# The causal mask of attention is added by a bf16 product instead of an fp32 product

## The reference

```
for blk in range(S // Q_BLOCK):            # two blocks of 128 queries
    q0 = blk * Q_BLOCK; q1 = q0 + Q_BLOCK
    s = einsum('bqhcd,bkhcd->bhcqk', q[:, q0:q1], k[:, :q1]) * ATTN_SCALE
    mask = arange(q1)[None, :] <= arange(q0, q1)[:, None]
    s = where(mask, s, -inf)
    a = softmax(s, axis=-1)
    a = a[:, :, 0] - lam * a[:, :, 1]      # 8 heads, two maps each
    outs.append(einsum('bhqk,bkhe->bqhe', a, v[:, :q1]))
```

## Time and profile before

| What | Value |
|---|---|
| Median of three executions | 1508.78 us |
| Lowest, highest | 1506.01, 1510.01 us |
| Profiled execution: span from first to last instruction | 1507.1 us (the page gives no other time of this execution) |
| Mean granted TensorE clock | 0.969 |
| TensorE busy (matmul, weight load) | 1451.4 us (96%), 1214.6 us (81%) |
| VectorE, ScalarE, GpSimd busy | 1156.3 us, 928.3 us, 129.1 us |
| DMA | 423.00 MB, mean 281 GB/s |

### The profile page before, as it was taken

How to read it: one execution, slowest core, us unless ns; L and a number is a source line. 1 busy time by engine, 2 the same in 40 slices (tenths; PEclk the granted TensorE clock), 3 DMA queues, 4 the chain that set the end, 5 groups by cost and what they waited for, 6 DMA issues and landing times.

```text
span 1507.1 us, 19735 instructions
## 1 busy us (share of the span) xinstructions
PE 1451.4 (96%) x7300; PEld 1214.6 (81%) x7300; DVE 1156.3 (77%) x894; ACT 928.3 (62%) x796; POOL 129.1 (9%) x129
## 2 busy tenths in 40 slices
PE   6789899999988999999999999999999999999998
PEld 5676689999877888888888888888888888888876
DVE  4764455444666888998988888898898889889875
ACT  4433443343445777777777767777777776777763
POOL 6650152000131000000000000000000000000000
PEclk9985699999999999999999999999999999999999
DMA  9440065555544997999999999999999999999970
GB/s 337 146 167 0 27 198 188 189 193 179 179 163 158 334 347 274 355 359 377 337 358 372 333 352 374 346 351 373 338 358 352 380 330 355 377 339 345 368 292 28
DMA packets 191374, 423.00 MB, mean 281 GB/s; under 512 B 6752, under 2 KB 30304, under 8 KB 191328
## 3 DMA queue, kind: packets, MB, share of 16 engines
q1 hardware_dynamic: 190880, 421.55, 78.2%
q0 software_dynamic: 448, 0.82, 0.2%
HBM read 421.30 MB, written 1.05 MB: 280 GB/s over the span
## 4 chain that ended last, share of the span: by engine, by line
PE 87%; DVE 6%; ACT 2%; POOL 2%; issue 1%; DMA 1%; SPq 0%; POOLq 0%; ACTq 0%; DVEq 0%
PE ps L264 26%; PE ps L266 25%; PE ps L265 25%; PE ps L732 2%; DVE w_lo L235 2%; PE ps L541 2%; PE ps L611 2%; PE ps L543 1%; POOL rstd L1476 1%; ACT w_hi L229 1%; PE ps L748 1%; DVE wide L1167 1%; DVE xs L1085 1%; DMA raw<-in_attn_w_qkv_dram 1%; ACT y_hi L1014 0%
## 5 line engine op out<-in xcount | busy, mean ns | idle before, releaser
L235 DVE TENSOR_TENSOR w_lo<-raw,w_hi 128x2048 fp32r<-128x2048 f32 (+1 forms) x393 | 881.1, 2257 | 210.5 <-ACT w_hi L229 209.5
L229 ACT ACTIVATE w_hi<-raw 128x2048 fp32r<-128x2048 f32 x393 | 752.1, 1916 | 201.6 <-PE ps L266 199.0
L264 PE MATMUL ps<-w_hi,xe_hi 128*128 128x512 f32 x896 | 356.2, 398 | 1.8 <-DVE w_lo L235 1.8
L266 PE MATMUL ps<-w_hi,xe_lo 128*128 128x512 f32 x896 | 350.3, 391 | 0.0
L265 PE MATMUL ps<-w_lo,xe_hi 128*128 128x512 f32 x896 | 349.9, 390 | 0.0
L264 PE MATMUL ps<-w_hi,h_t_hi 128*128 128x512 f32 x536 | 210.6, 393 | 3.4 <-DVE h_t_lo L1250 1.8
L266 PE MATMUL ps<-w_hi,h_t_lo 128*128 128x512 f32 x536 | 209.1, 390 | 0.0
L265 PE MATMUL ps<-w_lo,h_t_hi 128*128 128x512 f32 x536 | 208.9, 390 | 0.0
L264 PEld LDWEIGHTS ps<-w_hi,xe_hi 128*128 128x128 f32 x896 | 168.9, 188 | 38.0 <-DVE w_lo L235 5.0
L266 PEld LDWEIGHTS ps<-w_hi,xe_lo 128*128 128x128 f32 x896 | 168.6, 188 | 36.1
L265 PEld LDWEIGHTS ps<-w_lo,xe_hi 128*128 128x128 f32 x896 | 169.0, 189 | 33.2
(11 more groups left out here) (215 smaller groups left out, 1382.2 us busy)
## 6 DMA issues: line engine op xcount, KB each, us to landing
raw<-in_moe_w_gate_dram SPq DMA_DIRECT2D x112, 1024.0 KB, 7.0
raw<-in_moe_w_down_dram SPq DMA_DIRECT2D x111, 1024.0 KB, 6.9
raw<-in_moe_w_up_dram SPq DMA_DIRECT2D x110, 1024.0 KB, 7.1
raw<-in_attn_w_qkv_dram SPq DMA_DIRECT2D x12, 1024.0 KB, 15.8
raw<-in_ffn_w_gate_dram SPq DMA_DIRECT2D x11, 1024.0 KB, 5.3
raw<-in_ffn_w_up_dram SPq DMA_DIRECT2D x11, 1024.0 KB, 5.4
raw<-in_ffn_w_down_dram SPq DMA_DIRECT2D x11, 1024.0 KB, 5.0
raw<-in_ple_w_gate_dram SPq DMA_DIRECT2D x8, 1024.0 KB, 7.8
```

What stands on the lines that cost most here:

```text
L229: nc.scalar.activation(w_hi[:, u % SPLIT, :], raw_slot(u), ACT.Copy).then_inc(hi_ready, 1)
L235: nc.vector.tensor_tensor(w_lo[:, u % SPLIT, 0:n], raw_slot(u)[:, 0:n], w_hi[:, u % SPLIT, 0:n].bitcast(F32), ALU.subtract).then_inc(lo_re ...
L264: nc.tensor.matmul(out, x[0], w[0], start=first, stop=False)
L266: return nc.tensor.matmul(out, x[1], w[0], start=False, stop=last)
```

## The change

The two fp32 operands of the mask product are replaced by bf16 copies of the same matrices. The fp32 identity stays for all transposes. GpSimd makes the bf16 mask in place of the fp32 one and a bf16 identity besides; an unused fp32 constant of ones goes.

```
-        ones = sb("ones", [P, P])
+        ident16 = sb("ident16", [P, P], BF16)
-        causal = sb("causal", [P, P])
+        causal16 = sb("causal16", [P, P], BF16)
...
-                return nc.tensor.matmul(ps[:, i % BUFS, at + nk - P:at + nk], ident[:, :], causal[:, :],
+                return nc.tensor.matmul(ps[:, i % BUFS, at + nk - P:at + nk], ident16[:, :], causal16[:, :],
                                         start=False, stop=True)
...
-            nc.gpsimd.memset(ones[:, :], 1.0)
             nc.gpsimd.memset(ones16[:, :], 1.0)
-            nc.gpsimd.memset(causal[:, :], 0.0)
+            nc.gpsimd.memset(causal16[:, :], 0.0)
...
-            nc.gpsimd.affine_select(out=causal[:, :], in_=causal[:, :], compare_op=ALU.is_ge, fill=MASKED, base=0,
+            nc.gpsimd.affine_select(out=causal16[:, :], in_=causal16[:, :], compare_op=ALU.is_ge, fill=MASKED, base=0,
                                     pattern=[[-1, P]], channel_multiplier=1)
+            nc.gpsimd.affine_select(out=ident16[:, :], in_=ones16[:, :], compare_op=ALU.is_equal, fill=0.0, base=0,
                                     pattern=[[-1, P]], channel_multiplier=1)
```

More of the change, by code:

```diff
@@ L1461, in _ @@
                                     pattern=[[-1, P]], channel_multiplier=1)
-            nc.gpsimd.affine_select(out=causal[:, :], in_=causal[:, :], compare_op=ALU.is_ge, fill=MASKED, base=0,
+            nc.gpsimd.affine_select(out=causal16[:, :], in_=causal16[:, :], compare_op=ALU.is_ge, fill=MASKED, base=0,
+                                    pattern=[[-1, P]], channel_multiplier=1)
+            nc.gpsimd.affine_select(out=ident16[:, :], in_=ones16[:, :], compare_op=ALU.is_equal, fill=0.0, base=0,
                                     pattern=[[-1, P]], channel_multiplier=1)
```

## The result

The changed kernel takes 1495.23 us (median of four; 1494.25 to 1496.52), the kernel before 1508.64 us beside it: a ratio of 0.9912, with a 95% interval of 0.99 to 0.9924, so 13.4 us less. Forecast were 9.4 us less and 1499.5 us. Direction and place were right; the size was short by 4 us, and the time lies 0.3 us under the low end of the range.

The account below looks back on a forecast made before the run. TensorE alone was taken to bound attention, at 1.2 GHz. Savings of 7.6 us (26 mask products) and 1.8 us (six others) made 9.4 us, from the 1508.8 us median to 1499.5 us; range 1495.5 to 1504.

Parts of the forecast that it names:

- The drain ahead of L543: Emptying the array between the 64-row scores and the 128-row mask product: 0.14 us, said to stay with bf16.
- The later constants of GpSimd: At the start, constants come about 0.1 to 0.2 us later; said to cost nothing, 0.2 us if uncovered.
- the 26 products followed by L564 or L580: Mask products of map 1, steps 2 to 15, and map 0, steps 4 to 15: 0.29 us less each, 7.6 us.
- The bf16 load, 0.08: Bare load of the bf16 mask's weights at 1.2 GHz, taken as 0.08 us, between nothing and 0.16.
- The next load, 0.21: The fp32 load behind the mask product needs 0.21 us and finds cover of only 0.11.
- the other six: Mask products followed by L541, both maps of steps 0 and 1, map 0 of 2 and 3: 1.8 us less.
- My upper bound: With the next load free as well, 0.40 us less for each of 26 mask products: 12.2 us in all.
- (a): Clock comes back later after attention, slowing the output projection: net 3 to 4.6 us lost, 1502.5 to 1504; chance 0.15.
- (b): Clock rises within attention: 12 us more would go, 1487 us; chance 0.05.
- (c): Only the mask product's second pass goes, its load costing as before: 6.9 us less, 1502 us; chance 0.17.
- (d): Changing data type around the mask product drains the array as changing rows does: 12.3 against 9.4, 1511.7 us; chance 0.03.
- (e): The bf16 mask product is run in two passes as well: 1508 us; chance 0.01.

Follow-up runs that it names:

- 128-row kernels: Score products padded with zeroed q rows to all 128 rows: the changed kernel so altered took 1480.13 us, the kernel before (fp32 mask) so altered 1480.78 us.

## Why the prediction was right and wrong

**Right.** TensorE bounds the loop at 1.2 GHz, and what goes off TensorE comes off the time: it is busy for 31.42 of 31.42 us after, and none of VectorE, ScalarE and the PSUM banks took over. The drain ahead of L543 stayed, the number of records halved (32), the clock stayed low, and what follows moved along. The later constants of GpSimd cost nothing that can be seen: the first L541 starts at 107.00 against 107.19. The Trainium skill, page "TensorEngine Tiling (Array Packing)", Key Properties, says that a change of the tiling mode drains the TensorE. The 128-row kernels agree: two passes of the scores take 0.42 us there instead of 0.73.

**The step that failed** is the price of the 26 products followed by L564 or L580, "0.08 + max(0.11, 0.21) = 0.29 us", a saving of 0.29 each. Measured are 0.08 ahead of L580 and 0.19 ahead of L564. Two of its terms were too large.

1. *The bf16 load, 0.08.* I had scaled the difference of two load records. The start times show 0.01 (118.80 and 118.81), since the next load may set off at once. Here a record's length was read as its price, against my own rule to go by starts. (The pitch of 0.08 is shorter than the mask's own stream of 0.11, so how it divides into load and stream is not shown; the sum is.)
2. *The next load, 0.21.* I took the pitch of full-array passes for it. But behind a change of rows that load is bare, and I had read a bare load as 0.16 a paragraph earlier. For L564 it is 0.16, for a transpose 0.06 (the kernel without a mask), and it is due with or without a mask. The stream of the mask, 0.11, lies beside it, so the mask adds only 0.02 to 0.03. Where rows don't change, the max(0.11, 0.21) holds: a mask ahead of L578 costs 0.21 in the 128-row kernel.

So the mask with its successor's delay costs 0.08 + 0.11 = 0.19 ahead of L564, whose second pass comes 0.11 late, and 0.08 ahead of L580, instead of 0.59 in both cases. The sum that the runs give is 12 x 0.40 + 14 x 0.50 = 11.8 us, where I had 7.6, and 1.8 to 2.2 for the other six (first four steps, 107.19 to 117.34 us before and 107.00 to 113.95 after, so 3.2 us, or 2.8 in the second profile of the changed kernel, less the 1.0 of their two L580), where I had 1.8. Together 13.6 to 14.0, measured 13.4 by the medians and 13.9 within attention by the profiles. My upper bound used 0.40 for all 26, for want of the transposes' short load. And the low end of the range, 1495.5, was not what its terms give: 1496.6 less 1.5 is 1495.1.

**Rivals.** (a), the clock coming back later, didn't happen: full clock from 159.00 to 171.50 us, one low stretch behind it as before. (b), the clock rising in the loop, didn't happen with this change; it did when the 64-row products went. (c), only the second pass, is out: it wanted 0.37 from the mask to its successor, and 0.08 is measured. (d), a drain between types, is out: 0.08 us between the two. (e) is out by the 32 records. The Trainium skill, page "TensorE: Matmul & The Clock Gate", had pulled two ways. Its section on LDWEIGHTS has a load's time go by columns alone; the loads of 128 columns here don't agree (bare 0.16 us for fp32 and 0.06 for its transpose, and 0.01 from the bf16 load to the next). Its table on Fast Weight Load has a full load that isn't fp32 measured about twice as fast; the load records of the mask in the two 128-row kernels agree, with medians of 0.099 us in bf16 and 0.191 in fp32.

**Open.** The kernels with no mask and with one mask product for both maps gain some 2 us more than their steps explain. In their profiles the output projection has no stretch of low clock, in the changed kernel's two profiles it has one of 3.4 us (some 1.6 us of loss). From its first product to the fillers behind it the projection takes 26.2 us before, in the changed kernel (twice), with the mask twice and with bf16 for map 0, and 24.6 to 25.1 with no mask, with one mask product (with and without fillers) and with fp32r. With L564 left between the maps the stretch lies at 160 to 163 us, just ahead of the projection. Most kernels have one profile, so even whether it goes with the kernel or with the execution is not shown.

## What to carry to other kernels

Price a product by what it does to the start of the next two, not by its own record: behind a change of the row count somebody's weights load bare, and a bf16 product put first hides there nearly for free (0.035 us), while without a change of rows it costs its stream (0.11 us), and ahead of an fp32 product it squeezes that one's load besides (0.21 us in all). Before making such a product cheaper, ask whether the change of rows itself can go: padding the 64-row scores with zeros to 128 rows gave 15 us more and made the type of the mask all but indifferent. Fewer drains and the higher clock share in these 15 us; no run separates them.

## What the runs showed that was not expected

- By the starts, a transpose's weights load bare in 0.06 us at the low clock, those of an fp32 product of the same size in 0.16.
- With 64-row products between the others the clock stood at 1.2 GHz for 48 us (after) to 61 us (before), though TensorE's records leave hardly a gap. With 128-row products alone it rose within the loop in both kernels (at 118.7 us with the bf16 mask, at 113.4 with the fp32 mask) and held 2.4 GHz to the end of the loop, with TensorE busy for 81 to 88% of 125 to 142 us. Whether the rows or something that goes with them decides this, no run shows. A busy share near 100% in the records doesn't say that the clock will be granted.
